# A two-block transformer kernel on one NeuronCore: GpSimd's modulation sums in pairs with more drains, and the load of the column sums moved behind the load of the out weights

## The reference

```python
def adaln(cond, mod_w, mod_b):
    m = jax.nn.silu(cond) @ mod_w + mod_b          # mod_w: (2, 1024, 6144)
    return jnp.split(m, 6, axis=-1)

def modulate(x, gain, shift, scale):
    return rms_norm_2(x, gain) * (1 + scale) + shift
```

## Time and profile before

| | us |
|---|---|
| median of 3 runs | 1932.02 (1929.85 to 1933.09) |
| the profiled execution, its own time | 1927.03 |
| its span, first to last instruction | 1925.0 |
| PE busy in the span | 1890.3 (98%) |
| DVE busy | 763.1 (40%) |
| ACT busy | 542.9 (28%) |
| POOL busy | 791.0 (41%) |
| POOL's products (L397), 448 of them | 274.1 |
| POOL's additions (L401 and L403), 392 of them | 287.9 |
| mean granted TensorE clock | 0.994 of 2.4 GHz |

### The profile page before, as it was taken

One profiled execution on the slowest core, in us unless ns is written; L12 is line 12 of the kernel. 1 busy time (PEld: TensorE's weight loads), 2 busy tenths in 40 slices (PEclk: granted clock), 3 DMA queues, 4 the chain that ended last, 5 costly groups with the idle time before them and its releaser, 6 DMA issues.

```text
span 1925.0 us, 26160 instructions
## 1 busy us (share of the span) xinstructions
PE 1890.3 (98%) x9828; PEld 1013.1 (53%) x9828; DVE 763.1 (40%) x1646; ACT 542.9 (28%) x1187; POOL 791.0 (41%) x1091
## 2 busy tenths in 40 slices
PE   9999999999999999999999999999999999999999
PEld 6645456556556545565555455664543444445433
DVE  1544543433220444343337463633453411234524
ACT  3143332123411244431225231651211222012110
POOL 1767767667675666767540012760111100001111
PEclk9999999999999999999999999999899999998999
DMA  7332342333535344242423422313699822055998
GB/s 295 118 110 100 110 169 97 118 140 110 178 142 165 107 148 161 99 167 88 163 114 115 148 83 87 121 63 157 249 386 375 339 101 88 0 218 193 381 370 320
DMA packets 70299, 322.16 MB, mean 167 GB/s; under 512 B 8680, under 2 KB 11174, under 8 KB 55590
## 3 DMA queue, kind: packets, MB, share of 16 engines
q1 hardware_dynamic: 41688, 216.22, 29.7%
q0 software_dynamic: 25328, 92.81, 14.0%
q10 hardware_dynamic: 3168, 11.54, 1.5%
HBM read 287.51 MB, written 33.03 MB: 167 GB/s over the span
## 4 chain that ended last, share of the span: by engine, by line
PE 92%; DVE 3%; DMA 1%; ACT 1%; issue 1%; DVEq 1%; POOL 0%; POOLq 0%; SPq 0%; ACTq 0%
PE psA L462 25%; PE psA L1859 10%; PE psA L454 9%; PE psA L2006 7%; PE psA L1900 6%; PE psA L627 6%; PE psSO L2025 4%; PE psT L441 3%; PE psA L503 3%; PE psSO L532 3%; PE psSO L542 2%; PE psSO L565 1%; PE psSO L2215 1%; PE psSO L600 1%; PE psT L1975 1%; PE psSO L2240 1%
## 5 line engine op out<-in xcount | busy, mean ns | idle before, releaser
L462 PE MATMUL psA<-gB,pool_mem 128*128 128x512 f32 x1024 | 455.3, 597 | 0.0
L397 POOL TENSOR_TENSOR pool_mem<-pool_mem,cs 128x256 f32<-128x256 f32 x448 | 274.1, 644 | 129.8 <-DMA pool_mem<-in_mod_w 129.3
L462 PEld LDWEIGHTS psA<-gB,pool_mem 128*128 128x128 f32 x1024 | 189.5, 190 | 224.2 <-issue 224.2
L401 POOL TENSOR_TENSOR pool_mem<-pool_mem 128x256 f32<-128x256 f32 x336 | 246.5, 761 | 31.2 <-issue 23.2
L1859 PE MATMUL psA<-pool_mem 128*128 128x512 f32 (+1 forms) x528 | 209.0, 555 | 3.4 <-DMA pool_mem<-in_odd_w_in 1.5
L454 PE MATMUL psA<-pool_mem,gB 128*128 128x256 f32 (+2 forms) x768 | 189.6, 403 | 1.6 <-ACT gB L796 1.6
L1808 POOL DMA_INDIRECT pool_mem<-xs_scratch,idx x38 | 35.7, 939 | 333.5 <-DVE idx L2639 306.1
L454 PEld LDWEIGHTS psA<-pool_mem,gB 128*128 128x128 f32 x768 | 143.9, 190 | 43.5 <-issue 7.1
L1859 PEld LDWEIGHTS psA<-pool_mem 128*128 128x128 f32 x528 | 99.2, 190 | 106.6 <-issue 99.0
L2006 PE MATMUL psA<-pool_mem 128*32 128x512 f32 (+1 forms) x896 | 141.1, 593 | 0.0
L1900 PE MATMUL psA<-pool_mem 128*128 128x512 f32 x256 | 113.9, 595 | 0.8 <-issue 0.8
(11 more groups left out here) (359 smaller groups left out, 2454.6 us busy)
## 6 DMA issues: line engine op xcount, KB each, us to landing
pool_mem<-in_w_gu SPq DMA_DIRECT2D x32, 2048.0 KB, 11.1
pool_mem<-in_mod_w POOLq DMA_DIRECT2D x56, 1024.0 KB, 7.9
pool_mem<-in_w_dn SPq DMA_DIRECT2D x32, 1024.0 KB, 13.5
pool_mem<-in_w_qk SPq DMA_DIRECT2D x24, 1024.0 KB, 6.3
ys_scratch<-pool_mem ACTq DMA_DIRECT2D x22, 512.0 KB, 10.6
pool_mem<-in_odd_w_in SPq DMA_DIRECT2D x5, 2048.0 KB, 9.8
pool_mem<-in_w_out SPq DMA_DIRECT2D x4, 2048.0 KB, 8.1
macc_scratch<-pool_mem POOLq DMA_DIRECT2D x56, 128.0 KB, 2.0
```

The source lines that it names most:

```text
L397: nc.gpsimd.tensor_tensor(wm[:, b, k], wm[:, b, k], c_all[:, k].to_broadcast([P, MCH]), ALU.mult)
L401: nc.gpsimd.tensor_tensor(wm[:, b, k], wm[:, b, k], wm[:, b, n + k], ALU.add)
L462: m = nc.tensor.matmul(psA[:, n % 2, :], w(i), src[:, k, :], start=(i == 0), stop=(i == len(ks) - 1))
```

## The change

Two things are changed, both in the first block.

In SP's queue the load of the first half of the out weights, with its wait, is moved ahead of the wait for `m_stored` and the first two column sums. This stands within the loop over layers; in layer 1 there are no column sums, and nothing is moved there.

In GpSimd's `multiply` the products are issued two at a time (rows k and k + 4), with a drain behind each two. The additions take two rows at once, 512 columns: rows 0 and 1 with 4 and 5 behind the third two products and ahead of their drain, rows 2 and 3 with 6 and 7 behind the last drain of the products, then rows 0 and 1 with 2 and 3, and last the addition of 256 columns into `macc` as before. A piece is now 12 operations and 7 drains, again 19 instructions.

```diff
+                sp.wait_ge(pa_ready, base + pa_qk(3, 1, 1) + 1)
+                load(OUT_SLOT[0], d["w_out"][L, 0], KD * 512)
                 if L + 1 == DEPTH:
                     sp.wait_ge(m_stored, 16 * (MACC // MCH))
                     sums_in(0)
                     sums_in(1)
-                sp.wait_ge(pa_ready, base + pa_qk(3, 1, 1) + 1)
-                load(OUT_SLOT[0], d["w_out"][L, 0], KD * 512)
                 sp.wait_ge(pa_ready, base + pa_v(3, 3) + 1)
...
             def multiply(b, row, loaded):
                 pool.wait_ge(m_loaded[b], loaded)
                 c_all = cs[:, row * KD:(row + 1) * KD].rearrange("p (k o) -> p k o", o=1)
-                for k in range(KD):
+
+                def times(k):
                     nc.gpsimd.tensor_tensor(wm[:, b, k], wm[:, b, k], c_all[:, k].to_broadcast([P, MCH]), ALU.mult)
+
+                def plus_two(k, n):
+                    low, high = (wm[:, b, a:a + 2].rearrange("p k n -> p (k n)") for a in (k, n + k))
+                    nc.gpsimd.tensor_tensor(low, low, high, ALU.add)
+
+                for k in range(4):
+                    times(k)
+                    times(4 + k)
+                    if k == 2:
+                        plus_two(0, 4)
+                    pool.drain()
+                plus_two(2, 4)
                 pool.drain()
-                for n in (4, 2):
-                    for k in range(n):
-                        nc.gpsimd.tensor_tensor(wm[:, b, k], wm[:, b, k], wm[:, b, n + k], ALU.add)
-                    pool.drain()
+                plus_two(0, 2)
+                pool.drain()
                 nc.gpsimd.tensor_tensor(macc[:, b], wm[:, b, 0], wm[:, b, 1], ALU.add)
                 pool.drain()
```

## The result

The change makes the kernel slower: 1954.64 us, the median of 4 runs (1950.44 to 1957.11), against 1930.93 us before (4 runs: the three named above and one of 1922.91); the ratio is 1.0122, 95% interval 1.0092 to 1.0152. The forecast was 1927.7 us with a range of 1923.5 to 1935. The profiled execution took 1956.09 us (span 1954.0) where that of before took 1927.03.

The account below looks back on a forecast made before the run. PE was taken to bound the kernel. Removing a 2.64 us stall and 1.72 us of low clock, with other terms about 0, gave -4.36 from the runs' median of 1932.02: 1927.7 us, range 1923.5 to 1935.

Parts of the forecast that it names:

- What bounds the kernel: Whole kernel: PE is busy for 1890.3 of 1925.0 us; GpSimd's modulation matters only through what it does to others.
- the three ways: GpSimd's modulation in the first block can matter through VectorE, through the DMA traffic, or by ending too late.
- The products in pairs: First-block rotations: drains behind each two products let VectorE in sooner, removing PE's stall and the low clock, -4.36 us.
- The wait at 199 us: PE's 2.64 us wait for ACT's division, behind a VectorE addition shut out during eight products; claimed to go.
- -4.36: Claimed gain in us near 199 us: the 2.64 us stall and 1.72 us of low clock behind it go.
- the 1.72 us of low clock: Time lost at the 1.2 GHz level behind PE's 2.64 us stall; claimed to go with that stall.
- the turn-taking at the latent rotation: VectorE's four additions at 88.78 us, alternating with GpSimd: taken as 0, bounds -1.28 and +2.8 us.
- The length of a piece: GpSimd's modulation pieces: 10.17 us against 10.15 before, +1 us over 56 pieces; bounds -39 and +80 us.
- The high bound: GpSimd's modulation with wide additions of 1.40 us and all gaps 0.34: 11.58 us a piece, +80 us.
- a late end: Modulation ends over 30.6 us later, so VectorE at the column sums stalls PE: 1948 us, chance 0.08.
- SP's queue: End of first block: out weights issued at about 986 us, sums after the stores, over 60 us of cover; cost 0.

Follow-up runs that it names:

- wide alone: Kernel before with SP's new order and 512-column additions, all eight products back to back with one drain behind them; 1926.01 us, ratio 0.998.
- six products: Changed kernel with its first drain behind six products and the next behind two products and a wide addition; 1926.21 us, ratio 0.9981.
- the order alone: Kernel before with only SP's out weights moved ahead of the column sums, GpSimd's modulation as before; 1932.8 us, ratio 1.0005.
- drains alone: Kernel before with SP's new order and drains behind the fourth, sixth and eighth product, additions of 256 columns as before; 1933.53 us, ratio 1.0032.
- both loads in: Changed kernel with GpSimd waiting for both loads of a turn before its first product; 2009.75 us, ratio 1.0394.
- the old one: Changed kernel with SP's order undone, column sums ahead of the out weights as before; 1953.59 us, ratio 1.0113.

## Why the prediction was wrong

**What bounds the kernel.** Right: PE bounds it, and the modulation acts only through others. The prediction named the three ways and then priced the wrong one as the likeliest.

**The products in pairs.** The mechanism held. VectorE, if it meets the start of a run of products, is shut out to the run's end: 5.11 to 5.21 us behind eight, 4.01 behind six, 2.3 to 3.05 behind four, 1.3 to 1.9 behind two. The wait at 199 us is gone in every trace of a changed GpSimd stream. That the pairs took it away isn't shown: it is also gone with eight products in a run (wide alone), where the meeting moved to 408 us and cost PE nothing. Against the trace before, -4.36 was right: between 190 and 210 us the changed kernel gains 4.1 us on it, and six products 4.3. Over other executions its worth may be smaller, since the 1.72 us of low clock is missing in the trace of the order alone, where the wait itself recurs. And the turn-taking at the latent rotation, which I had set to 0 between -1.28 and +2.8, cost +1.7 us at 92 us and +1.35 us at 647 us, with 3.5 us of half clock behind the first. I had bounded one place of this kind and not counted the second, in layer 2, where GpSimd happened to be out of the way before. At 92 us the four additions (L1057, before L1046) took 5.37 us in place of 4.01: two of them, beside wide additions, 1.65 us each, where each had taken 1.0 beside products. The whole gain goes there. What sets those waits isn't settled: they are 0.3 to 2.5 us in layer 2 over eleven traces, above 1 us with wide additions alone as with drains alone, and 0.3 us with both in the version of six products, so the phase between the engines is a better guess than any one edit, and no more than a guess.

**The length of a piece.** This is the step that failed. "A gap is 0.14 or 0.34. I take ... 0.2 for the three gaps behind products alone": the wide additions were right (1.27 us taken, 1.269 at the median), so were the gaps of 0.14, and the first gap in a piece was 1.98 us in first and 0.41 us in second pieces, 2.33 and 0.67 at the mean, where I had put 0.2. I had taken the cost of a drain from drains that had nothing to wait for but their own engine. The high bound, 0.34 a gap and +80 us, held the measured +53 us, but by its number and not by its reason: it took high prices for everything. The turn of two pieces grew by 1.77 us in its first and 0.59 us in its second (the wide additions gave some of the gaps back), less 0.5 us between turns; 28 turns of 1.85 us make 52 of the 53 us. The 0.34 of a first piece against 0.14 elsewhere, which I treated as scatter, was no sign of this wait: with both loads in, the same gap is still 0.34 to 0.43 us, and what it waits for is open. What the trace before did hold against me are its four first pieces whose load landed late, with gaps of up to 2.56 us; I had priced all pieces by the first one.

**The rival "a late end".** It was the true one, with a chance of 0.08. Its path (VectorE at the column sums, PE behind it) and its point were right: the stores may be 30.6 us later than 990.46, which is 35.1 us behind the end of the queries and keys, and the runs show 35.8. From there, 53.0 - 30.6 = 22.4 us of stall would have been said, and 20.9 were measured. What made the modulation late was not what it named: it took wide additions of 1.40 us and gaps of 0.24, where these were 1.27 and 0.14 and one drain a piece waited for a DMA. That it came close to the time (1948 us) is so far luck.

**SP's queue.** Right: cost 0 both ways (1.0005 with the new order alone, 1953.59 against 1954.64 us with the old one). The out weights went out at 986.78, as said.

**The sum.** For the two profiled executions: stall at the sums 20.9, half clock behind it 2.7, the two latent rotations 1.7 + 1.7 + 1.35, the wait and its low clock at 199 us -4.4; together 24. ScalarE's instructions, the same 1187 in both traces, are 24.3 us later than before at the end of the first block, so nothing there is left over. The difference of the executions is 29.1 us. The other 4.8 us come in the second block, where nothing was changed: 1.9 between 1350 and 1450 us of the trace before, 2.1 between 1500 and 1550, and 0.8 behind 1850. The 3.4 us at the low clock at 1557.7 make 1.7 of it; the rest isn't explained. In the traces of the nine experiments the second block took from 0.3 us less to 5.3 us more than before, so it differs between executions by as much; the medians of the kernels differ by 23.7 us.

The Trainium skill's rule (SBUF — State Buffer, Who interferes with whom) that the shared port is an exclusive lock held for a whole instruction fits the turn-taking, where VectorE's and GpSimd's instructions alternate, VectorE's at about 1.0 us each beside products and 1.65 beside wide additions. It doesn't fit the meetings at the start of a run: there VectorE's instruction lasted over 8, 6, 4 or 2 of GpSimd's (5.20, 4.01, 2.87 and 1.74 us), until the next drain.

## What to carry to other kernels

A drain on GpSimd was here also a wait for GpSimd's own DMAs, so its price depends on what that engine has in flight: put drains where its loads and stores have landed, or put enough work ahead of them to cover the landing (here six products of 0.58 us for a load 2.9 us away). Work that runs beside the critical path has an end that somebody waits for: before lengthening a loop of 56 pieces, work out how many ns a piece may grow (here 550), and let no term of that size go unread. Price a gap from all its occurrences and not from the first piece: four of the 28 first pieces before had shown it at up to 2.56 us.

## What the runs showed of the hardware

- GpSimd's first drain of a piece ended 0.18 us (0.14 to 0.18) after the landing of a load that GpSimd had issued, and 0.08 us after that of a store, in every piece of the kernel after (28 and 28). DMAs issued by SP didn't hold it: SP's 2 MB of out weights, issued at 435.26 in the kernel after, landed at 443.59, and the drain that ended ahead of 442.85, with them in flight, cost 0.14 us (441.43 + 1.27 = 442.70 to 442.85) as the later ones did. GpSimd's own load that flew beside them landed 3.6 us behind the turn's first load, against 3.0 at the median, and the first gap of that piece was 2.65 us; that SP's load slowed it isn't shown:

```profile
435.26 0.33 SPq L250 DMA_DIRECT2D pool_mem<-in_w_out  x1
...
438.96 2.51 POOL L398 TENSOR_TENSOR pool_mem<-pool_mem,cs 128x256 f32<-128x256 f32 x4 [2.65 <-issue]
441.43 1.27 POOL L402 TENSOR_TENSOR pool_mem<-pool_mem 128x512 f32<-128x512 f32 x1
442.85 1.19 POOL L398 TENSOR_TENSOR pool_mem<-pool_mem,cs 128x256 f32<-128x256 f32 x2
```

  That loads issued by SP would free the first drain of a piece is likely by this, but wasn't tried.
- A VectorE instruction that starts within a store's issue on GpSimd (0.02 to 0.40 us ahead of the first product behind it), or up to 0.05 us behind the start of that product, can be shut out for the whole run; others that start there aren't. When it comes in the midst of a run, the two take turns. Why the first case doesn't also turn to taking turns is open.
- TensorE's granted clock fell to 0.50, the 1.2 GHz level, during the long stalls (for 23.9 us around one of 20.9, for 78.5 us around one of 76.1). Behind waits of 2.0 to 3.4 us in the first block it stood at that level for 3.4 to 6.9 us ten times, and not at all twice (2.65 us with the order alone, 2.0 with drains alone).
